# The context half of a norm moved into the down products before it, its latent half summed on TensorE, and a tree of block decays built ahead of the levels

## What is computed

```
def _rmsnorm(x, w):
    y = xf * lax.rsqrt(jnp.mean(xf * xf, axis=-1, keepdims=True) + EPS)
    return (y * w).astype(x.dtype)
...
    # end of the first block: layer 1, latents alone, then the final norm
    xl = xl + 0.5 * g3l * swiglu(modulate(rmsnorm(xl, norm_w[2]), sh3l, sc3l), w_ffn2_in, w_ffn2_out)
    return rmsnorm(xl, final_norm_w)
...
    # start of the second block: x is the result above, ctx an input of its own
    pl = _modulate(_rmsnorm(xl, norm1_w[l]), sh1, sc1) @ w_in[l]
    pc = _modulate(_rmsnorm(xc, norm1_w[l]), sh1c, sc1c) @ w_in[l]
...
def _hgrn_scan(q, k, v, lf, S):      # in chunks of the tokens, decays exp(cumsum lf)
    b = jnp.cumsum(fc, axis=2)
    a = jnp.einsum('bhtk,bhtsk,bhsk->bhts', qc, jnp.exp(rel), kc)
    o = jnp.einsum('bhts,bhsv->bhtv', a, vc) + jnp.einsum('bhtk,bhkv->bhtv', qc * jnp.exp(b), S)
```

## Time and profile before

| what | us |
|---|---|
| runs of the kernel before, three | 2249.58, 2245.12, 2254.86 |
| their median | 2249.58 |
| the profiled execution, its own time | 2246.66 |
| its span in the trace | 2244.9 |
| PE busy in the span | 2139.7 (95%) |
| DVE busy | 1505.2 (67%) |
| ACT busy | 863.5 (38%) |
| POOL busy | 130.3 (6%) |

### The profile page before, as it was taken

The page is one execution under the profiler, slowest core; times in us unless marked ns, Lnnn a source line. Parts: engine busy times, 40 slices in busy tenths (PEclk is TensorE's granted clock), DMA queues, the critical chain, the costliest instruction groups (busy, mean ns, idle before and its releaser), DMA issues.

```text
span 2244.9 us, 29011 instructions
## 1 busy us (share of the span) xinstructions
PE 2139.7 (95%) x11464; PEld 1802.0 (80%) x11464; DVE 1505.2 (67%) x2597; ACT 863.5 (38%) x1447; POOL 130.3 (6%) x104
## 2 busy tenths in 40 slices
PE   5999999998999999999999999899997999889998
PEld 3888888874788888888888888579996888778888
DVE  3777777757577775656476556777545676658984
ACT  3432222425452222243322225455445355533233
POOL 1000000015000000000000000310001000010001
PEclk8999999999999999999999999999997999999999
DMA  6455555330135555535455543336553232024444
GB/s 259 178 189 199 201 175 202 127 104 24 57 131 188 188 197 204 198 118 180 163 196 188 203 163 123 103 113 228 186 200 106 100 113 94 1 95 150 153 150 148
DMA packets 61415, 342.11 MB, mean 152 GB/s; under 512 B 6624, under 2 KB 8672, under 8 KB 31584
## 3 DMA queue, kind: packets, MB, share of 16 engines
q1 hardware_dynamic: 60096, 338.56, 43.1%
q10 hardware_dynamic: 1184, 1.70, 0.2%
HBM read 339.19 MB, written 1.05 MB: 152 GB/s over the span
## 4 chain that ended last, share of the span: by engine, by line
PE 88%; DVE 7%; ACT 2%; issue 1%; DMA 1%; POOL 0%; SPq 0%; DVEq 0%; ACTq 0%; POOLq 0%
PE bank L565 46%; PE bank L573 23%; PE bank L1053 7%; PE bank L639 3%; PE bank L650 1%; DVE w_lo L1589 1%; DMA raw<-stream 1%; PE bank L862 1%; PE bank L883 1%; DVE arena L2046 1%; ACT w_hi L1103 1%; DVE arena L2128 1%; DVE small L1963 1%; PE bank L844 1%; PE bank L1031 0%
## 5 line engine op out<-in xcount | busy, mean ns | idle before, releaser
L1589 DVE TENSOR_TENSOR w_lo<-raw,w_hi 128x1024 fp32r<-128x1024 f32 (+1 forms) x389 | 469.2, 1207 | 514.1 <-ACT w_hi L1103 512.7
L1103 ACT ACTIVATE w_hi<-raw 128x1024 fp32r<-128x1024 f32 (+1 forms) x389 | 403.5, 1037 | 1018.1 <-PE bank L565 1010.4
L565 PE MATMUL bank<-hidden_hi,w_hi 128*128 128x512 f32 (+1 forms) x1392 | 492.4, 363 | 2.5 <-ACT w_hi L1103 2.5
L565 PE MATMUL bank<-hidden_lo,w_hi 128*128 128x512 f32 (+1 forms) x1392 | 492.3, 363 | 0.0
L565 PE MATMUL bank<-h_hi,w_hi 128*128 128x512 f32 (+1 forms) x1416 | 461.3, 343 | 6.2 <-ACT w_hi L1103 4.7
L565 PE MATMUL bank<-h_lo,w_hi 128*128 128x512 f32 (+1 forms) x1416 | 459.0, 341 | 0.0
L1622 DVE CUSTOM_DVE_ANT_0 scratch<-columns_raw,late,params 128x1024 f32<-128x1024 f32 x288 | 360.2, 1280 | 5.7 <-issue 5.3
L573 PE MATMUL bank<-hidden_hi,w_lo 128*128 128x512 f32 (+1 forms) x1392 | 308.3, 363 | 1.9 <-DVE w_lo L1589 1.9
L565 PEld LDWEIGHTS bank<-h_hi,w_hi 128*128 128x128 f32 x1416 | 269.5, 190 | 38.1 <-ACT w_hi L1103 4.0
L565 PEld LDWEIGHTS bank<-hidden_hi,w_hi 128*128 128x128 f32 x1392 | 263.5, 189 | 43.8 <-issue 2.9
L565 PEld LDWEIGHTS bank<-hidden_lo,w_hi 128*128 128x128 f32 x1392 | 263.7, 189 | 40.5
(11 more groups left out here) (278 smaller groups left out, 1979.4 us busy)
## 6 DMA issues: line engine op xcount, KB each, us to landing
raw<-stream SPq DMA_DIRECT2D x229, 1024.0 KB, 5.0
columns_raw<-columns_in SPq DMA_DIRECT2D x176, 512.0 KB, 3.7
x<-x_in SPq DMA_DIRECT2D x1, 2048.0 KB, 9.3
late<-cond_in SPq DMA_DIRECT2D x2, 1024.0 KB, 5.8
x<-ctx_in ACTq DMA_DIRECT2D x1, 1024.0 KB, 5.9
out<-x SPq DMA_DIRECT2D x2, 512.0 KB, 3.0
late<-consts_in ACTq DMA_DIRECT2D x1, 640.0 KB, 3.8
consts<-consts_in SPq DMA_DIRECT2D x1, 464.5 KB, 3.9
```

The source lines that it names most:

```text
L565: last = nc.tensor.matmul(acc, w_hi[:, buffer, kc, :], v(first_chunk + kc), start=start and kc == n == 0, stop=False)
L1103: nc.scalar.activation(w_hi[:, buffer, 0:chunks, :], raw[at % RING][:, 0:chunks, sub * P:(sub + 1) * P], ACT.Copy)\
L1589: nc.vector.tensor_tensor(w_lo[:, buffer, 0:chunks, :], raw[at % RING][:, 0:chunks, sub * P:(sub + 1) * P], w_hi[:, buffer, 0:chunks, :].b ...
```

## The change

Three things are changed, and one renaming goes with them.

1. **The context half of norm_a moves into `down("21")`.** In steps 1 to 4 ACT squares two context chunks each into the free half of `arena`; POOL adds the eight (seven additions of 256 columns); at the start of unit 5 (step 10) PE makes one product of `ones` with the sum; in step 11 ACT takes the root (with a table load), in step 12 DVE makes the modulation factors and the reciprocal over 256 columns; in steps 13 to 20 DVE scales a chunk each, in steps 15 to 22 ACT modulates and rounds it, in steps 16 to 23 DVE makes its rest. The joint product waits for the eight (`ctx_ready`).
2. **norm_a handles latents alone, and POOL has no part in it.** ACT squares 256 columns per chunk, PE sums each by a product with `ones` over 256 columns as it comes; ACT takes the root of one row (1 x 256), two small products turn it into columns, DVE takes the reciprocal, and PE spreads it by two products with `ident`. The scaled diagonal is gone.
3. **The tree of block decays** is built in one go at the end of `projections()` (`later_totals`, six operations), each level in a place of its own, and `join_totals` is gone from the levels.
4. Several semaphores that existed once per layer are now one each, with counts that go on; their waits stand at the same places. These lines are left out below.

```diff
-        NORMS += [("final1", 3 * DEPTH, CTX), ("norm_a", 3 * DEPTH + 1, 0), ("norm_b", 3 * DEPTH + 2, CTX),
+        NORMS += [("final1", 3 * DEPTH, CTX), ("norm_a", 3 * DEPTH + 1, CTX), ("norm_b", 3 * DEPTH + 2, CTX),
...
-            return KC - 1 if name in DELAYED else ADDED - 1
+            return KC - 1 if name in DELAYED else 0 if name == "norm_a" else ADDED - 1
...
-        hg_totals = scratch[:, 1:3, :]
+        hg_totals = [scratch[:, 1:3, :].rearrange("p d t -> p (d t)"), rms]
+        for level in range(2, LEVELS):
+            at, n = T - (2 * P * MH >> level - 1), 2 * P * MH >> level
+            hg_totals.append(rinv[:, at:at + n])
...
+        border_squares = [arena[:, kc, 0:CTX] for kc in range(KC)]
+        ctx_h = [arena[:, KC + kc, 0:CTX] for kc in range(KC)]
+        ctx_rms, ctx_rinv, rms_row = arena[:, 2 * KC, 0:CTX], arena[:, 2 * KC + 1, 0:CTX], arena[0:1, 2 * KC + 2, 0:CTX]
+        CTX_SQUARES, CTX_RMS, CTX_RINV, CTX_SCALED, CTX_HIGH, CTX_LOW = 1, 11, 12, 13, 15, 16
+        CTX_SUM = 5
...
+            def border_norm_sum(name):
+                n, t0 = NORM_AT[name], START[name]
+                for kc in range(KC):
+                    pe.wait_ge(sem("square_ready"), KC * n + kc + 1)
+                    last = nc.tensor.matmul(bank[SUM_BANK][:, 0:LAT], ones, border_squares[kc], start=kc == 0, stop=kc == KC - 1)
+                    if kc == 0:
+                        last.then_inc(half_begun, 1)
+                last.then_inc(sem("norm_summed"), 1)
+                At.norms = n + 1
+                pe.wait_ge(sem("rms_ready"), n + 1)
+                for tc in range((T - t0) // P):
+                    last = nc.tensor.matmul(bank[SUM_BANK][:, CTX + tc:CTX + tc + 1], rms_row[:, tc * P:(tc + 1) * P], ones[0:1, 0:1],
+                                            start=True, stop=True, skip_group_check=True)
+                last.then_inc(sem("rms_turned"), 1)
+                pe.wait_ge(sem("diag_ready"), diags_before(name) + (T - t0) // P)
+                for tc in range((T - t0) // P):
+                    last = nc.tensor.matmul(bank[SPREAD_BANK][:, tc * P:(tc + 1) * P], norm_rinv[:, tc:tc + 1].broadcast_to([P, P]), ident,
+                                            start=True, stop=True, skip_group_check=True)
+                last.then_inc(sem("rinv_spread"), 1)
...
+                    if name == "21" and j == CTX_SUM:
+                        pe.wait_ge(sem("ctx_added"), KC - 1)
+                        nc.tensor.matmul(bank[SUM_BANK][:, 0:CTX], ones, border_squares[0], start=True, stop=True)\
+                            .then_inc(sem("ctx_summed"), 1)
...
+                pe.wait_ge(sem("ctx_ready"), KC)
...
-                norm_sum("norm_a")
+                border_norm_sum("norm_a")
...
+                if name == "norm_a":
+                    nc.scalar.activation(border_squares[kc], x[:, kc, t0:], ACT.Square).then_inc(sem("square_ready"), 1)
+                    return
...
+            def context_norm(n):
+                if n == CTX_SQUARES:
+                    act.wait_ge(sem("ctx2_loaded"), 16)
+                for kc in range(2 * (n - CTX_SQUARES), 2 * (n - CTX_SQUARES) + 2):
+                    if 0 <= kc < KC:
+                        nc.scalar.activation(border_squares[kc], x[:, kc, 0:CTX], ACT.Square).then_inc(sem("ctx_squared"), 1)
+                if n == CTX_RMS:
+                    act.wait_ge(sem("ctx_summed"), 1)
+                    nc.scalar.activation(ctx_rms, bank[SUM_BANK][:, 0:CTX], ACT.Sqrt, bias=const("eps"), scale=1.0 / D)\
+                        .then_inc(sem("ctx_rms"), 1)
+                kc = n - CTX_HIGH
+                if 0 <= kc < KC:
+                    act.wait_ge(sem("ctx_scaled"), kc + 1)
+                    s, b = modulation("norm_a", kc, 1)
+                    own.link(nc.scalar.activation(ctx_h[kc], ctx_h[kc], ACT.Identity, bias=b, scale=s))
+                    nc.scalar.activation(h_hi[:, kc, 0:CTX], ctx_h[kc], ACT.Copy).then_inc(sem("ctx_high"), 1)
...
-                nc.scalar.activation(norm_rms[:, 0:(T - t0) // P], bank[SUM_BANK][:, 0:(T - t0) // P], ACT.Sqrt, bias=const("eps"),
-                                     scale=1.0 / D).then_inc(sem("rms_ready"), 1)
+                target, sums = (rms_row, bank[SUM_BANK][0:1, 0:LAT]) if name == "norm_a" else \
+                    (norm_rms[:, 0:(T - t0) // P], bank[SUM_BANK][:, 0:(T - t0) // P])
+                nc.scalar.activation(target, sums, ACT.Sqrt, bias=const("eps", rows=1 if name == "norm_a" else P), scale=1.0 / D)\
+                    .then_inc(sem("rms_ready"), 1)
...
-                act.wait_ge(sem("ctx2_loaded"), 16)
...
-                dve.wait_ge(sem("rms_ready"), n + 1)
-                own.link(nc.vector.reciprocal(norm_rinv[:, 0:chunks], norm_rms[:, 0:chunks]))
-                for tc in range(chunks):
+                if name == "norm_a":
+                    dve.wait_ge(sem("rms_turned"), 1)
+                    nc.vector.reciprocal(norm_rinv[:, 0:chunks], bank[SUM_BANK][:, CTX:CTX + chunks]).then_inc(sem("diag_ready"), chunks)
+                else:
+                    dve.wait_ge(sem("rms_ready"), n + 1)
+                    own.link(nc.vector.reciprocal(norm_rinv[:, 0:chunks], norm_rms[:, 0:chunks]))
...
+            def context_norm(n):
+                if n == CTX_RINV:
+                    factors(2, 0, ("norm_a",))
+                    dve.wait_ge(sem("ctx_rms"), 1)
+                    own.link(nc.vector.reciprocal(ctx_rinv, ctx_rms))
+                if 0 <= n - CTX_SCALED < KC:
+                    kc = n - CTX_SCALED
+                    nc.vector.tensor_tensor(ctx_h[kc], x[:, kc, 0:CTX], ctx_rinv, ALU.mult).then_inc(sem("ctx_scaled"), 1)
+                if 0 <= n - CTX_LOW < KC:
+                    kc = n - CTX_LOW
+                    dve.wait_ge(sem("ctx_high"), kc + 1)
+                    nc.vector.tensor_tensor(h_lo[:, kc, 0:CTX], ctx_h[kc], h_hi[:, kc, 0:CTX].bitcast(F32), ALU.subtract)\
+                        .then_inc(sem("ctx_ready"), 1)
...
-                own.mark(nc.vector.tensor_tensor(hg_totals[:, d, :].rearrange("p (h n) -> p h n", h=MH), a[:, :, :, 0], a[:, :, :, 1], ALU.mult))
+                own.mark(nc.vector.tensor_tensor(hg_totals[0][:, d * MH * P:(d + 1) * MH * P].rearrange("p (h n) -> p h n", h=MH),
+                                                 a[:, :, :, 0], a[:, :, :, 1], ALU.mult))
+            def later_totals():
+                for level in range(1, LEVELS):
+                    parts = hg_totals[level - 1].rearrange("p (n two) -> p n two", two=2)
+                    own.link(nc.vector.tensor_tensor(hg_totals[level], parts[:, :, 0], parts[:, :, 1], ALU.mult))
...
+                        later_totals()
...
-                    return [hg_totals[:, d, :].rearrange("p (h n two b) -> p h n two b", h=MH, two=2, b=size // 2)[:, :, :, :, 0]
-                            for d in range(2)]
+                    of = hg_totals[size.bit_length() - 2].rearrange("p (d h n two) -> p d h n two", d=2, h=MH, two=2)
+                    return [of[:, d] for d in range(2)]
...
-                def join_totals(level):
-                    if level:
-                        for what in ("query", "key"):
-                            dve.wait_ge(sem(f"hg_{what}_updated"), level + 2)
-                        t = hg_totals.rearrange("p d (m two b) -> p (d m) two b", two=2, b=1 << (level - 1))[:, :, :, 0]
-                        own.mark(nc.vector.tensor_tensor(t[:, :, 0], t[:, :, 0], t[:, :, 1], ALU.mult))
...
-                    join_totals(level)
...
-                factors(2, 0, ("norm_a",))
-                dve.wait_ge(sem("ctx2_loaded"), 16)
...
+                if i == DEPTH - 1 and until is None:
+                    for kc in range(1, KC):
+                        pool.wait_ge(sem("ctx_squared"), kc + 1)
+                        if kc > 1:
+                            pool.wait_ge(sem("ctx_added"), kc - 1)
+                        nc.gpsimd.tensor_tensor(border_squares[0], border_squares[0], border_squares[kc], ALU.add).then_inc(sem("ctx_added"), 1)
...
-                pool.wait_ge(sem("ctx2_loaded"), 16)
-                add_squares("norm_a")
```

More of the change, by code:

```diff
@@ L785, in exchange @@
                         last = nc.tensor.matmul(bank[ROPE_BANK[1]][:, :], const("perm"), rope_parts[1], start=False, stop=True)
-                    last.then_inc(sem(f"exchanged{tag}"), 1)
+                    last.then_inc(sem("exchanged"), 1)
                 for n in range(16):
@@ L1328, in mla_and_conv @@
                         c = CONV_STEPS[i].index(n)
-                        act.wait_ge(sem(f"conv_gated{tag}"), c + 1)
-                        nc.scalar.activation(h_hi[:, 4 + c, t0:], squares[:, c, t0:], ACT.Copy).then_inc(sem(f"conv_high{tag}"), 1)
+                        act.wait_ge(sem("conv_gated"), 4 * i + c + 1)
+                        nc.scalar.activation(h_hi[:, 4 + c, t0:], squares[:, c, t0:], ACT.Copy).then_inc(sem("conv_high"), 1)
```

(12 more changed lines are left out.)

34 lines of the change are left out of this document (18 added, 16 removed).

## The result

| | median | range of the runs | to the kernel before |
|---|---|---|---|
| before | 2249.71 us | 2245.12 to 2257.08 (9 runs) | |
| after | 2237.13 us | 2233.59 to 2242.81 (9 runs) | 0.9938, 95% interval 0.9926 to 0.9951 |
| after, measured once more (`e_again`), beside other runs of before with a median of 2251.41 us | 2236.00 us | 2233.80 to 2240.11 (6 runs) | 0.9930, 0.9914 to 0.9946 |

By the medians the change saves 12.6 us in the first comparison and 15.4 in the second; the intervals of the ratios make 11.0 to 16.6 and 12.2 to 19.4. The forecast was 17.1 us and 2232, with a range of 2225 to 2240. The time is in the range, but the forecast was too good by some 4 us, and most of this has one place.

A forecast was written before the change was run, and what follows sets the result against it. The prediction held the kernel bound by PE's products, so only PE's idle stretches could be won: seam -14.6, added product +0.2, tree -2.7, together -17.1 us from the median 2249.58, giving 2232 (range 2225 to 2240).

The forecast's parts named there:

- First leg: Seam, from final1's last scaling to norm_a's first: that first scaling starts at about 1706.6 instead of 1718.31, 11.7 us less.
- the term of the sums: Seam: a product with ones costs 0.22 us, twice that at half clock; the last ends by 1703.9.
- The chain behind the sums: Seam, root to first scaling: small steps end at 1705.7, but DVE's conversions of w_hi and w_lo at 1706.6.
- Rival 1: Seam: the new chain of hand-overs at low PE clock sets the start, 2.1 us not covered; about 2235, chance 0.12.
- Second leg: Seam, norm_a's first scaling to the half after the joint product: 1718.5 instead of 1733.10; whole seam saves 14.6 us.
- without the low clock it would still do so: Seam: the saving of 14.6 us would also hold without PE's low clock.
- The added product: down("21"): the one product added on PE costs 0.22 us and counts in full, +0.2 in the sum.
- The step that was thought tightest for ACT: down("21"), step 11: conversion, table load and root take 2.7 us in 2.16; conversion ends 0.6 late, still hidden.
- Rival 4: down("21"): DVE and ACT, waiting for each other, hold up PE; 19 us given back, 2252, slower; chance 0.03.
- rival 3: Joint product: the next weights, issued only at its start, land late; 3 us come back, 2236; chance 0.03.
- The tree: HGRN levels: without joins a period takes 3.70 us, saving 2.7 us over six periods; range 2.0 to 3.0.
- Rival 2: HGRN levels keep their pace, bound by PE's scores or ACT's merge; costs the 2.7 us: 2235, chance 0.08.

The follow-up runs named there:

- e_ones_r: Kernel after, with the eight latent squares and a copy of the ones in fp32r, one pass per product: 2236.61 us, ratio 0.9926 to before.
- e_warm: Kernel after, plus 19 products that nobody reads in the gaps where PE waits at the seam: 2232.01 us, ratio 0.9912 to before.

## Why the prediction was right, and where it was wrong

**First leg: the term of the sums was mis-sized.** "A product of this kind costs 153.7 / 704 = 0.22 us at full clock and twice that at half" took the 704 for products. The loop at L1053 makes 22 pairs of 16 products, 352; the 704 are records, two to a product, as the 16 records of L695 for eight products show. The price is 0.44 at full clock and, by 6.57 / 8, 0.82 with most of them at half. A product of the same size in fp32r is 0.12, so the fp32 one costs nearly four of them. That is what the Trainium skill states ("FP8 and Floating Point Precision", section "TensorE Precision Notes": true FP32 takes four passes through the array); the trace agrees, 0.44 beside 4 x 0.12 = 0.48, and it shows the four passes as two records. Weighed against the 0.22, that page would have shown the slip before the run. The prediction knew the clock would be at half, so with the right price it would have had eight products of some 0.8 against squares 0.40 apart: 3.2 us late. "PE all but keeps up: to 1703.9", which is 1.2 after final1's last scaling, was measured as 4.3. These 3.1 us are most of the error.

**The chain behind the sums was right.** 2.7 us were given from the sums' end to the first scaling, 2.6 were measured. As forecast, w_lo stands directly ahead of the scaling and hides the small products. Rival 1 put its 2.1 us there and gives nearly the measured time, but not for the reason that it names; only in `e_ones_r` does the spread become the last to arrive, by 0.19.

**Second leg: 11.9 forecast, 12.93 measured.** The pace of a chunk was 0.99, better than the 1.11 of the earlier trace rows, and the last h_hi came 7.8 after the first scaling (8.9 forecast). But PE set the end. The prediction gave half clock 3.3 us of the joint product, by the earlier trace rows; it had 5.2 (1716.49 to 1721.7), as the clock had risen during the sums and fell again behind them. Half of the 1.9 us more is 0.9. Another 0.26 was left out: the conversion for the next half is released only in the joint product's last part, after 40 of its 48 products (1726.56 in the chain), and PE waits for it at 1727.76. That "without the low clock it would still do so" is borne out: at full clock (`e_warm`) the second leg is 11.19, and the seam saves 15.1.

**down("21").** The added product cost 0.43, not 0.22, by the same misreading. Everything else hid as reckoned: PE shows no wait between 1637 and 1702. The step that was thought tightest for ACT, with the table load, reads

```profile
1667.59 1.06 ACT L1139 ACTIVATE w_hi<-raw 128x1024 fp32r<-128x1024 f32 x1 [1.31 <-PE bank L575]
1668.66 1.28 ACT L1175 ACT_TABLE_LOAD   x1
...
1669.96 0.47 ACT L1175 ACTIVATE arena<-bank,consts 128x256 f32<-128x256 f32 x1
1670.33 1.05 ACT L1139 ACTIVATE w_hi<-raw 128x1024 fp32r<-128x1024 f32 x1
```

and stayed clear. Rival 4 did not come about. Nor did rival 3: had the next weights come late, the way from the seam to level 0 would be longer, and it is 166.29 beside 166.28 before.

**The tree: 2.7 forecast, 3.2 measured.** A level lasts 3.63, not 3.70. The 3.0 at the upper end had room for a copy that overlaps the last multiplication, and was still too low. The six periods fell from 24.93 to 21.78 by their starts (1895.43 to 1917.21). Rival 2 did not come about: in the new levels PE waits 1.6 us for a copy of DVE in each of the last six periods of 3.63.

**The sum.** With the prices as measured it is -10.5 + 0.4 - 3.2 = -13.3, beside -12.6 and -15.4 by the medians. The mechanism and the signs held everywhere. The error of 3.8 is 3.1 from the first leg and 1.0 from the second, 0.2 from the added product, and 0.5 the other way from the tree. None of the misses that the range was made for came about, so that it held the time is in part luck. The sum was also made against the profiled execution of before, whose end, as it turned out, was 2.5 us better than that of most others.

## What to carry to other kernels

Before a group's busy time is divided by its count for the price of an operation, compare the count with the number of times that the code's loop runs: a product here had two records. Where the trace shows an engine at a lower clock behind idle gaps, price the chain behind them at that clock, and expect it to change when the gaps do: here the clock set both the pace of the sums and that of the product behind them, and 19 products of no use in the gaps gave back more (4.6 us of the seam, 2.8 beside `e_again`) than the cheaper form of the product did (3.1, and 1.4). And when two traces are compared for effects of 0.1%, cut them at common points first: two stretches far from the change moved the profiled span by 4.1 + 2.5 us and hid half of the effect.

## What the runs showed that was not expected

- An fp32 product of 256 columns is two records and takes 0.44 us at full clock, 0.82 with the clock at half for most of eight; the same product in fp32r is one record, and kept up with squares 0.40 apart at half clock.
- Four products of one column, the turn of the root's row, take 0.60 us at full clock and 1.01 at half, and four of 128 columns 0.71 and 1.22.
- With PE kept busy by products that nobody reads, the granted clock stayed at 1.00 over the whole seam, where in the kernel after it was at 0.50 for 13.6 us.
- Where the clock stands at half in the rest of the kernel differs from execution to execution of the same code, and is worth 0 to 4.1 us in one attention and up to 2.6 us behind the levels. The seam of one code took 18.12 and 19.90 us.
